# W_in converted by column groups with a scale each, block 0's gate projections moved into its attention, W_out converted in block 1

## The chip, the cores and the metric

The kernel runs on one core of one Trainium2 chip. The metric is the device time of one execution in microseconds, the median of several runs; lower is better. 3 runs of the kernel before stand at 1543.43 to 1545.45 us, with a median of 1544.86.

## The reference, cut to what matters

One layer of a decoder trunk over SEQ = 4096 tokens of width 1024: a norm, one input projection whose columns feed three mixers, gates, one output projection, a residual and a final norm.

```python
def rmsnorm(x, g):
    return x * rsqrt(mean(x * x, -1) + 1e-6) * g
...
h = rmsnorm(x, norm_g)                       # (4096, 1024)
proj = h @ w_in                              # 1024 x 2576
q_g, k_g, v_g, gk_lr, gate_g, u_p, gate_p, q_m, gate_m = split(proj)
gk = log_sigmoid(gk_lr @ w_gk_up + b_gk) / 16
o_gla = rmsnorm(gla_chunked(q_g, k_g, v_g, gk), gla_norm_g) * silu(gate_g)
o_pool = (multiscale_pool(u_p) @ pool_w per group) * pool_scale * silu(gate_p)
o_mem = memory_attention(q_m, rmsnorm(mem, mem_norm_g), w_mem_kv) * silu(gate_m)
x = x + concat(o_gla, o_pool, o_mem) @ w_out # 1024 x 1024
return rmsnorm(x, final_g)
```

gla_chunked is gated linear attention in chunks of 64 tokens, 4 heads; multiscale_pool is a trailing mean over 2, 4, 8 and 16 tokens; memory_attention attends to 256 memory tokens, 4 heads. All inputs and the output are float32.

## The kernel before, in words

**Numbers.** The large products run on float16 parts. A float32 matrix is scaled by a power of two, its float16 rounding is the high half, the rest is the low half, and three matmuls (high by high, high by low, low by high) replace one (`split`, L324 to L331). The scale comes from the largest entry: VectorE reduces along the columns, GpSimd's `partition_all_reduce` takes the largest over the partitions, and VectorE's `exponents` (L792) makes the scale and its inverse from the exponent bits.

**The head, L237 to L257, L293 to L322, L567 to L631, L807 to L853, L1115 to L1175.** SyncE issues all loads on one queue: the small vectors, the memory tokens and W_mem (1 and 2 MB), the transposed u columns of W_in, pool_w in four pieces, then W_in in eight slices of 128 rows. TensorE folds pool_w into the u columns. ScalarE squares the memory tokens, GpSimd adds the squares up, and VectorE scales the tokens. VectorE reduces each slice of W_in as it lands (L816) and, with the norm's weights `g_in` multiplied in (L828), one scale `s_w` for the whole of W_in comes out (L832). Only then ScalarE writes the high half of slice after slice (`hi_tile`, L593, 2560 columns each) and VectorE the low half (L852). The norm weights are part of the scaled W_in (`gs`, L837), so that x is only multiplied by its reciprocal root mean square. x of block 0 comes after the memory keys and values (L252 to L254), since `xb0` takes their buffer. W_out is loaded whole (4 MB, L257) when block 0's x has been split.

**The blocks.** 4096 tokens in 16 blocks of 256 (`TB`). `run_blocks` (L227) writes block 0 and block 15 out and runs blocks 1 to 14 in a loop, on each engine its own instruction stream; the order within an engine is the order of the code, and semaphores join the engines. TensorE's order in a block (L367): low-rank gate and q (L380, L384), decay logits (L388), k, v (L399), then `features` for the GLA gates, u, memory q, pool gate and memory gate (L403 to L411), 48 matmuls of 256 columns each; then the attention part: transposes and scores (L425, L435), memory scores (L452), states (L463), turns of the memory probabilities (L476), head outputs (L484, L490), memory values (L541), head norms (L498). Between the pieces of attention stand four quarters of the output projection of the block before (`quarter`, L501, `out_proj`, L345); block 0 has none. Within attention `rms_sum`, ScalarE's `rstd` and `x_parts`, VectorE's `normalise` (L799) and GpSimd's `x_lo_of` (L1137) make the next block's x.

**W_out in block 0.** VectorE reduces it (L940), GpSimd joins the partitions (L1171), and ScalarE (L679) and VectorE (L952) split it in eight slices, while TensorE runs block 0's projections. The raw copy `woraw` lies outside the buffers of the blocks.

**GpSimd's order** (L1114 on): constants, the memory tokens' sums (L1134), two all-reduces (L1149, L1151), the sums of x's squares, the low-rank weights (L1157 to L1161), x times its scale (L1164), the low half of x (L1143), memsets, the third all-reduce (L1171), memsets, then in each block the pooling sums (L1184 to L1191), the squares' sums and the low half of the next x.

```python
        def wait_split(eng, k):
            eng.wait_ge(hi_w, k + 1)
            eng.wait_ge(lo_w, k + 1)
```

Of the kernel before, what the change touches and what calls it, by code (L numbers as in the profile page):

```python
# [19 lines left out]
ALU = mybir.AluOpType  # L20
# [8 lines left out]
P = 128  # L29
D = 1024  # L30
# [40 lines left out]
O_TAIL = DIN * KT * 4  # L71


def hybrid_block(nc, xt, x, memt, w_in, w_ut, w_gk_up, vecs, pool_w, counts, w_mem, w_out, final_g, out):
    NB = xt.shape[0]
    ctx = ExitStack()
    with ctx:
# [21 lines left out]
        sca = sb("sca", [P, 34], F32)  # L99
# [5 lines left out]
        wmx = sb("wmx", [P, 2, KT], F32)  # L105
# [5 lines left out]
        g_in, g_mem, b_gk, g_out = vec[:, 0:8], vec[:, 8:16], vec[:, 16:18], vec[:, 18:26]  # L111
# [46 lines left out]
        wraw = view(0, [KT, DIN], F32)  # L158
        woraw = view(O_TAIL, [KT, D], F32)
        xb0 = view(O_TAIL, [KT, TB], F32)  # L160
        sq0 = view(O_TAIL + 8192, [KT, TB], F32)
        memb = view(O_TAIL, [KT, NMEM], F32)
        wmraw = view(O_TAIL + 8192, [KT, 512], F32)
        wflat = whl[:, :, :, :].rearrange("p a b c -> p (a b c)").bitcast(F32)
        wut = wflat[:, 0:2048].rearrange("p (a b) -> p a b", a=2)
        pwb = wflat[:, 2048:2304].rearrange("p (a b) -> p a b", a=2)
        msq = wflat[:, 2304:2304 + KT * NMEM].rearrange("p (a b) -> p a b", a=KT)
        rmem = wflat[:, 4608:4608 + NMEM]

        bank = [ctx.enter_context(nc.psum_tensor(f"bank{i}", [P, 512], F32)) for i in range(8)]  # L170
        kraw = bank[1][:, :].rearrange("p (a b) -> p a b", a=NPAIR)
        vraw = bank[2][:, :].rearrange("p (a b) -> p a b", a=MT)
# [3 lines left out]
        def col(n):  # L176
            return sca[:, n:n + 1]
        s_w, i_w, s_o, i_o, s_m, i_m, sc_in, sc_q, sc_out = (col(n) for n in range(9))
        s_vk, i_vk, e_vk, m_vk = (sca[:, n:n + 2] for n in (22, 24, 26, 28))
        s_v, s_k, i_v, i_k = (col(n) for n in (22, 23, 24, 25))  # L180
        sc_ms, sc_neg = col(30), col(31)
        gs = sca[:, 12:20]
        e_tmp = col(20)
        m_tmp = col(21)


        d_vec, d_mem, d_wut, d_wout, d_x, d_res, d_store = (
            sem(n) for n in ("d_vec", "d_mem", "d_wut", "d_wout", "d_x", "d_res", "d_store"))
        d_w = [sem(f"d_w{k}") for k in range(KT)]

        cleared, built, ident_ok, mem_sq, mem_sum, mem_ms, mem_ln, mem_r, mem_n = (
            sem(n) for n in ("cleared", "built", "ident_ok", "mem_sq", "mem_sum", "mem_ms", "mem_ln", "mem_r", "mem_n"))
        memk_done, memv_done, fold_done, fold_out = (
            sem(n) for n in ("memk_done", "memv_done", "fold_done", "fold_out"))
        max_in, max_all, hi_w, lo_w, hi_v, lo_v, hi_k, lo_k, hi_o, lo_o, scaled = (
            sem(n) for n in ("max_in", "max_all", "hi_w", "lo_w", "hi_v", "lo_v", "hi_k", "lo_k", "hi_o", "lo_o",
                             "scaled"))
        low_rank, qm_hi, qm_lo = (sem(n) for n in ("low_rank", "qm_hi", "qm_lo"))

        pe_lr, pe_q, pe_k, pe_logit, pe_v, pe_p2, pe_out, pe_ket, pe_sc, pe_ms, pe_st, pe_rb, pe_pt, pe_o, pe_msq, pe_pv = (  # L200
            sem(n) for n in ("pe_lr", "pe_q", "pe_k", "pe_logit", "pe_v", "pe_p2", "pe_out", "pe_ket", "pe_sc",
                             "pe_ms", "pe_st", "pe_rb", "pe_pt", "pe_o", "pe_msq", "pe_pv"))

        lr_out, abs_ok, expabs, softplus, eb_ok, enb_ok, ebl_ok, v_out, p2_out, y_sq, y_ln, y_r, x_sq = (
            sem(n) for n in ("lr_out", "abs_ok", "expabs", "softplus", "eb_ok", "enb_ok", "ebl_ok", "v_out",
                             "p2_out", "y_sq", "y_ln", "y_r", "x_sq"))
# [15 lines left out]
        def wait_split(eng, k):  # L222

            eng.wait_ge(hi_w, k + 1)
            eng.wait_ge(lo_w, k + 1)

        def run_blocks(eng, step, tail):  # L227

            step(0, True, False)
            with eng.Fori(1, NB - 1) as i:  # L230
                step(i, False, False)
            step(NB - 1, False, True)
            tail(NB)

        @block.sync
        def _(sp):
            sp.dma_start(vec[:, 0:26], vecs).then_inc(d_vec, 16)  # L237
            sp.dma_start(cnt[:, :, :], counts).then_inc(d_vec, 16)
            for g in range(P // RANK):
                sp.dma_start(up4[g * RANK:(g + 1) * RANK, :], w_gk_up).then_inc(d_vec, 16)  # L240
            sp.dma_start(fg[:, :], final_g.partition_broadcast(P)).then_inc(d_vec, 16)
            sp.dma_start(memb, memt).then_inc(d_mem, 16)
            sp.dma_start(wmraw, w_mem).then_inc(d_mem, 16)
            sp.dma_start(wut, w_ut).then_inc(d_wut, 16)
            sp.wait_ge(cleared, 1)
# [9 lines left out]
            sp.wait_ge(x_hi, 2)  # L255
# [996 lines left out]
```

## Time and profile before

| | |
|---|---|
| median of 3 runs | 1544.86 us (1543.43 to 1545.45) |
| the profiled execution, span | 1543.8 us |
| outside the span, median less span | 1.1 us |
| TensorE busy | 1443.0 us, 93% of the span |
| VectorE busy | 724.0 us, 47% |
| ScalarE busy | 608.1 us, 39% |
| GpSimd busy | 236.4 us, 15% |
| mean granted TensorE clock | 0.973 |
| read and written | 52.20 and 16.78 MB |

The span runs from the first to the last instruction of one profiled execution. PE is TensorE, PEld its weight loads, DVE VectorE, ACT ScalarE, POOL GpSimd, SP SyncE. A number in square brackets behind an instruction is the time its engine stood idle ahead of it, with what ended that; "issue" there is time in which the engine waited for nothing that the profile shows. A busy share is a mean over stages with different limits, so the stages are read one by one.

### The profile page before, as it was taken

What the parts mean: (1) busy time and instruction counts of PE and PEld (TensorE: products, weight loads), DVE (VectorE), ACT (ScalarE), POOL (GpSimd) and SP (SyncE); (2) the same over time, 40 slices, a digit from 0 to 9 for tenths busy, and PEclk for the clock granted to TensorE, in tenths of its full rate; (3) what the DMA queues carried; (4) which work ended last, traced back from release to release, by engine and by line L of the source; (5) the groups of instructions that cost most, each with busy time, mean ns of one, the idle gap of its engine ahead of it and who ended that gap; (6) DMA issues with size and microseconds to landing.
All of it is one profiled execution on the core that took longest, in us unless ns stands there. A gap on an engine that the chain in (4) does not pass through costs nothing.

```text
span 1543.8 us, 28261 instructions
## 1 busy us (share of the span) xinstructions
PE 1443.0 (93%) x11746; PEld 1046.2 (68%) x11746; DVE 724.0 (47%) x1221; ACT 608.1 (39%) x1101; POOL 236.4 (15%) x217
## 2 busy tenths in 40 slices
PE   3359699999999999999999999999999999999996
PEld 2238476776867677676867677686867767686762
DVE  2876625436172535527163544627163543616253
ACT  1344425344342534434252534434262534434241
POOL 1231201121110201121020202121020112112000
PEclk9669799999999999999999999999999999999998
DMA  8130100102010010102001010202001010201001
GB/s 337 65 136 1 42 2 28 54 0 82 0 69 12 27 54 10 71 0 82 0 36 46 27 54 0 82 0 82 0 27 54 21 61 0 82 0 46 10 28 68
DMA packets 15432, 69.32 MB, mean 45 GB/s; under 512 B 2352, under 2 KB 2480, under 8 KB 12848
## 3 DMA queue, kind: packets, MB, share of 16 engines
q1 hardware_dynamic: 15408, 68.98, 11.9%
q8 instruction: 18, 0.29, 0.1%
q14 instruction: 6, 0.05, 0.0%
HBM read 52.20 MB, written 16.78 MB: 45 GB/s over the span
## 4 chain that ended last, share of the span: by engine, by line
PE 90%; DVE 4%; ACT 2%; DMA 1%; issue 1%; POOL 1%; SPq 1%; DVEq 0%; ACTq 0%; POOLq 0%
PE bank L330 75%; PE bank L484 2%; PE bank L452 2%; PE bank L490 2%; PE bank L476 2%; PE bank L498 2%; DVE whl L852 1%; PE bank L541 1%; DVE wmx L816 1%; PE bank L463 1%; PE bank L388 1%; DMA whl<-in_pool_w 1%; PE bank L435 1%; PE bank L380 1%; POOL arena L1134 1%
## 5 line engine op out<-in xcount | busy, mean ns | idle before, releaser
L330 PE MATMUL bank<-arena,whl 128*128 128x256 f16 x6144 | 684.6, 274 | 2.6 <-DVE whl L852 2.6
L330 PEld LDWEIGHTS bank<-arena,whl 128*128 128x128 f16 x6144 | 602.3, 98 | 84.1 <-issue 6.5
L330 PE MATMUL bank<-arena 128*128 128x512 f16 x1536 | 344.1, 381 | 6.4 <-DVE arena L872 6.4
L330 PEld LDWEIGHTS bank<-arena 128*128 128x128 f16 x1536 | 147.8, 98 | 181.3 <-issue 15.4
L963 DVE SCALAR_TENSOR_TENSOR arena<-arena 64x256 f32<-64x256 f32 x60 | 25.2, 420 | 314.6 <-POOL arena L1191 313.2
L330 PE MATMUL bank<-whl,arena 128*128 128x512 f16 x768 | 168.3, 379 | 0.0
L686 ACT ACTIVATE arena<-bank,sca 128x512 f32<-128x512 f32 x64 | 43.9, 688 | 254.4 <-PE bank L330 253.3
L330 PEld LDWEIGHTS bank<-whl,arena 128*128 128x128 f16 x768 | 75.2, 99 | 86.9
L1143 POOL TENSOR_TENSOR arena<-arena 128x1024 f16<-128x1024 f32 x32 | 77.8, 2451 | 285.7 <-ACT arena L621 285.7
L1134 POOL TENSOR_TENSOR arena<-arena 128x1024 f32<-128x1024 f32 (+2 forms) x48 | 76.7, 1599 | 231.7 <-ACT arena L599 222.6
L1184 POOL TENSOR_TENSOR arena<-arena 128x542 f32<-128x542 f32 x16 | 17.4, 1090 | 606.1 <-ACT arena L693 598.3
L1001 DVE TENSOR_REDUCE mx<-bank 128x2 f32<-128x512 f32 x64 | 41.1, 683 | 138.4 <-PE bank L452 138.4
L1013 DVE SCALAR_TENSOR_TENSOR arena<-arena,rsum 128x256 f16<-128x256 f32 x128 | 62.3, 538 | 58.1 <-ACT arena L738 58.1
L883 DVE SCALAR_TENSOR_TENSOR arena<-bank,sca,arena 128x512 f32<-128x512 f32 x64 | 47.8, 749 | 79.8 <-DMA arena<-in_x 58.5
L728 ACT ACTIVATE arena<-bank,nm,sca 128x256 f32<-128x256 f32 x128 | 71.2, 560 | 4.0 <-ACT nm L718 2.4
L738 ACT ACTIVATE arena<-arena,rsum 128x256 f16<-128x256 f32 x128 | 56.1, 498 | 25.8 <-DVE rsum L1007 25.8
L671 ACT ACTIVATE arena<-bank,sca 128x512 f32<-128x512 f32 x32 | 22.0, 687 | 102.7 <-PE bank L330 102.7
L872 DVE SCALAR_TENSOR_TENSOR arena<-arena,sca 128x2048 f16<-128x2048 f32 x16 | 37.6, 2351 | 51.2 <-ACT arena L637 51.2
L643 ACT ACTIVATE arena<-arena 128x1024 bf16<-128x1024 f32 x32 | 33.6, 1050 | 55.5 <-DVE arena L883 55.5
L1038 DVE COPY arena<-bank 128x1024 f16<-128x1024 f16 x64 | 43.9, 687 | 16.3 <-PE bank L476 16.2
L700 ACT ACTIVATE arena<-bank 64x512 f16<-64x512 f32 x32 | 18.9, 592 | 73.3 <-PE bank L330 72.9
L763 ACT ACTIVATE arena<-bank,eps 128x512 f32<-128x512 f32 x32 | 21.7, 678 | 59.0 <-PE bank L498 59.0
(154 smaller groups left out, 1467.9 us busy)
## 6 DMA issues: line engine op xcount, KB each, us to landing
arena<-in_xt SPq DMA_DIRECT2D x16, 1024.0 KB, 5.2
arena<-in_x SPq DMA_DIRECT2D x32, 512.0 KB, 3.3
out<-arena SPq DMA_DIRECT2D x32, 512.0 KB, 2.6
arena<-in_w_in SPq DMA_DIRECT2D x8, 768.0 KB, 16.1
arena<-in_w_out SPq DMA_DIRECT2D x1, 4096.0 KB, 12.2
arena<-in_w_in SPq DMA_DIRECT2D x8, 392.0 KB, 16.2
arena<-in_w_mem SPq DMA_DIRECT2D x1, 2048.0 KB, 11.0
arena<-in_memt SPq DMA_DIRECT2D x1, 1024.0 KB, 6.6
```

Of the source, the lines that this page charges most:

```text
L330: mm = nc.tensor.matmul(ap, lhs, rhs, start=k == 0 and n == 0, stop=(k, n) == last)
L643: nc.scalar.activation(junk, yb, ACT.Square, accum_out=ysum[:, 0:1]).then_inc(y_sq, 1)
L686: nc.scalar.activation(gate[:, g:g + 2, :], bank[b][:, :].rearrange("p (a t) -> p a t", a=2), ACT.Silu, scale=sc_in).then_inc(p2_out, 1)
L728: a = nc.scalar.activation(pr[n % 2][:, h, :], bank[2 + n % 2][:, h * 256:(h + 1) * 256], ACT.Exp, bias=nm[:, 2 * n + h:2 * n + h + 1], sc ...
L738: a = nc.scalar.activation(phl[n % 2][:, 0, h, :], pr[n % 2][:, h, :], ACT.Copy, scale=rsum[:, 2 * n + h:2 * n + h + 1])
L872: nc.vector.scalar_tensor_tensor(mhl[:, 1, :, :], mixed, s_m, mhl[:, 0, :, :], ALU.mult, ALU.subtract).then_inc(m_lo, 1)
L883: nc.vector.scalar_tensor_tensor(yb[:, c], bank[h][:, :], sc_out, yb[:, c], ALU.mult, ALU.add).then_inc(y_add, 1)
L1001: nc.vector.tensor_reduce(mx[:, 2 * n:2 * n + 2], bank[2 + n % 2][:, :].rearrange("p (h m) -> p h m", h=2), AX.X, ALU.max).then_inc(max_ok, 1)
L1013: a = nc.vector.scalar_tensor_tensor(phl[n % 2][:, 1, h, :], pr[n % 2][:, h, :], rsum[:, 2 * n + h:2 * n + h + 1], phl[n % 2][:, 0, h, :], ...
L1038: nc.vector.tensor_copy(pt[:, p, :, t * P:(t + 1) * P], b16[b].rearrange("p (a b) -> p a b", b=P)).then_inc(pt_out, 1)
L1134: nc.gpsimd.tensor_tensor(buf[:, 0:half, :], buf[:, 0:half, :], buf[:, half:2 * half, :], ALU.add).then_inc(signal, 1)
L1143: nc.gpsimd.tensor_tensor(xn[:, 1, k, :], whole[:, k, :], xn[:, 0, k, :], ALU.subtract).then_inc(x_lo, 1)
```

## The change

Seven column groups of W_in (Q with the low-rank columns, K, V, memory Q, u, GLA gates, pool and memory gates) are seven inputs, loaded by one DMA each, reduced, scaled and split one by one. Each has its own scale, and each result is multiplied by its own inverse. The weights of the norm are no longer in W_in: `normalise` multiplies them into x, eight instructions on VectorE instead of one. The raw groups lie in buffers that the blocks use later, so that x of block 0 is loaded at once. The head's sums of squares move from GpSimd to VectorE. GpSimd takes the low halves of three groups, whose raw copy ScalarE scales in place first, and all-reduces each group's largest entry.

Block 0 no longer projects its four gates in the projection part: they stand at the places of the four quarters in its attention (`first_gate`), are copied out unscaled by silu (`raw_gate`), and one silu over all of them follows. W_out is loaded whole behind block 0's last weights for its largest entry alone, and in block 1, now written out as well (`second`), loaded again in eight tiles through two buffers that lie in `mixed`, and split there. The reserved size of a scratch area for DMAs, a build argument, is set to 2048.

```diff
-            for k in range(KT):
-                sp.dma_start(wraw[:, k, 0:CU], w_in[:, k, 0:CU]).then_inc(d_w[k], 16)
-                sp.dma_start(wraw[:, k, CGP:DIN], w_in[:, k, CU:DIN - 256]).then_inc(d_w[k], 16)
-            sp.wait_ge(memk_done, 1)
-            sp.wait_ge(memv_done, 1)
-            sp.dma_start(xb0, xt[0]).then_inc(d_x, 16)
...
+            sp.dma_start(memb, memt).then_inc(d_mem, 16)
+            sp.dma_start(wmraw, w_mem).then_inc(d_wmem, 16)
+            sp.dma_start(xb, xt[0]).then_inc(d_x, 16)
+            sp.dma_start(rq, w_q).then_inc(d_wq, 16)
+            sp.dma_start(rk, w_k).then_inc(d_wk, 16)
+            sp.dma_start(wut, w_ut).then_inc(d_wut, 16)
+            sp.dma_start(rv, w_v).then_inc(d_wv, 16)
+            sp.dma_start(rqm, w_qm).then_inc(d_wqm, 16)
+            sp.dma_start(rg, w_g).then_inc(d_wg, 16)
...
+            wait_weights(sp, GV)
+            sp.dma_start(rp, w_p).then_inc(d_wp, 16)
...
+                if first:
+                    wait_weights(sp, GG)
+                    wait_weights(sp, GP)
+                    sp.dma_start(woraw, w_out).then_inc(d_wout, 16)
+                if second:
+                    sp.wait_ge(m_lo, 1)
+                    for k in range(KT):
+                        if k >= 2:
+                            sp.wait_ge(hi_o, k - 1)
+                            sp.wait_ge(lo_o, k - 1)
+                        sp.dma_start(wotile[k % 2], w_out[:, k, :]).then_inc(d_tile[k % 2], 16)
```

On TensorE, in block 0, the fold of pool_w stands behind the logits, and the gates in attention:

```diff
+                if first:
+                    fold_pool()
+                    wait_weights(pe, GK)
...
+                def first_gate(n):
+                    if first:
+                        wait_weights(pe, GG if n < 2 else GP)
+                        if n >= 2:
+                            pe.wait_ge(gate_out, n - 1)
+                        features(n % 2, GATES[n]).then_inc(pe_g, 1)
 
                 mem_scores(0)
                 mem_scores(1)
...
                 quarter(0)
+                first_gate(0)
                 mem_scores(2)
                 mem_scores(3)
```

On ScalarE (in block 0's stream: Q, x, K, then V behind the low-rank copy, the fold's copies, U, the memory values, QM, GG, GP):

```diff
+            def weights_hi(g, c, raw, parts):
+                act.wait_ge(w_scaled, g + 1)
+                w, n = raw.shape[2], KT // parts
+                for h in range(parts):
+                    k = slice(n * h, n * (h + 1))
+                    a = nc.scalar.activation(whl[:, 0, k, c:c + w], raw[:, k, :], ACT.Copy, scale=sw[:, g:g + 1])
+                    if g in LO_POOL:
+                        a = nc.scalar.activation(raw[:, k, :], raw[:, k, :], ACT.Copy, scale=sw[:, g:g + 1])
+                    a.then_inc(hi_w, 1)
...
+                for k in range(3):
+                    out_hi(k)
+                if first:
+                    act.wait_ge(fold_done, 4)
+                    weights_hi(GG, CG, rg, 2)
+                else:
+                    silu(1, 2, 0)
+                    out_hi(3)
+                    out_hi(4)
+                    silu(2, 3, 2)
+                    out_hi(5)
+                    out_hi(6)
...
+                raw_gate(2)
+                raw_gate(3)
+                if first:
+                    act.wait_ge(gate_out, 4)
+                    nc.scalar.activation(gate, gate, ACT.Silu).then_inc(silu_ok, 1)
+                    nc.scalar.preload_act_table_set(EXP_LN)
```

On VectorE:

```diff
             def normalise(n):
                 dve.wait_ge(rb_ok, n + 1)
-                r = sq[:, 1:2, :].broadcast_to([P, KT, TB])
-                nc.vector.tensor_tensor(xb, xb, r, ALU.mult).then_inc(xn_ok, 1)
+                for k in range(KT):
+                    a = nc.vector.scalar_tensor_tensor(xb[:, k, :], xb[:, k, :], gx[:, k:k + 1], sq[:, 1, :],
+                                                       ALU.mult, ALU.mult)
+                    if k % (KT // 2) == KT // 2 - 1:
+                        a.then_inc(xn_ok, 1)
...
+                if first:
+                    dve.wait_ge(fold_out, 4)
+                    nc.vector.tensor_reduce(w_top[:, GU:GU + 1], ru, AX.XY, ALU.max,
+                                            apply_absolute_value=True).then_inc(w_max, 1)
+                    weights_scale(GQM, AR_QM)
...
+                    weights_scale(GU, AR_U)
+                    weights_max(GG, rg, d_wg)
+                    weights_lo(GU, CU, ru)
...
+                    weights_scale(GG, AR_GG)
+                    weights_max(GP, rp, d_wp)
+                    weights_scale(GP, AR_GP)
+                if second:
                     dve.wait_ge(d_wout, 16)
+                    after(nc.vector.tensor_reduce(wmx[:, :], woraw, AX.X, ALU.max, apply_absolute_value=True))
...
+                    dve.wait_ge(max_all, AR_WO)
                     exponents(mmax[:, 2:3], s_o, i_o)
+                    nc.vector.tensor_scalar(o_gain, o_gain, s_o, None, ALU.mult).then_inc(o_scaled, 1)
+                    dve.wait_ge(o_scaled, 1)
+                if not first:
+                    mixed_lo(i - 1)
+                if second:
                     for k in range(KT):
                         dve.wait_ge(hi_o, k + 1)
```

On GpSimd:

```diff
+            all_max(AR_G, sca[:, 87:88], g_top)
+            all_max(AR_Q, w_all[:, GQ:GQ + 1], w_top[:, GQ:GQ + 1])
             x_lo_of(0)
+            all_max(AR_K, w_all[:, GK:GK + 1], w_top[:, GK:GK + 1])
+            all_max(AR_V, w_all[:, GV:GV + 1], w_top[:, GV:GV + 1])
+            all_max(AR_KV, kvmax[:, 2:4], kvmax[:, 0:2])
...
+            all_max(AR_QM, w_all[:, GQM:GQM + 1], w_top[:, GQM:GQM + 1])
+            all_max(AR_U, w_all[:, GU:GU + 1], w_top[:, GU:GU + 1])
+            pool.wait_ge(fold_done, 4)
+            weights_lo(CQM, rqm, 0, KT, HI_DONE[GQM])
+            all_max(AR_GG, w_all[:, GG:GG + 1], w_top[:, GG:GG + 1])
+            weights_lo(CG, rg, 0, KT // 2, HI_DONE[GG] - 1)
+            weights_lo(CG, rg, KT // 2, KT, HI_DONE[GG])
+            all_max(AR_GP, w_all[:, GP:GP + 1], w_top[:, GP:GP + 1])
...
+                if second:
+                    all_max(AR_WO, mmax[:, 2:3], mmax[:, 0:1])
+                pool.wait_ge(u_out, i + 1)
...
+                if first:
+                    weights_lo(CGP, rp, 0, KT // 2, HI_DONE[GP] - 1)
+                    weights_lo(CGP, rp, KT // 2, KT, HI_DONE[GP])
```

## Rows read from the trace of the kernel before

**Rows 1.** The page: busy time of each engine, its share of the span, instructions

```profile
PE 1443.0 (93%) x11746; PEld 1046.2 (68%) x11746; DVE 724.0 (47%) x1221; ACT 608.1 (39%) x1101; POOL 236.4 (15%) x217
```

**Rows 2.** Busy time by stretch: PE, PEld, DVE, ACT, POOL, clock, DMA share, GB/s

```profile
0.00:92.00 92.00, 23.62 (x100) 20.12 (x100) 54.76 (x48) 32.67 (x26) 28.91 (x27) 0.75 0.43 169
92.00:185.50 93.50, 77.21 (x632) 59.31 (x633) 57.87 (x94) 38.63 (x66) 15.24 (x17) 0.88 0.14 57
273.00:361.00 88.00, 88.00 (x731) 63.92 (x730) 40.02 (x71) 35.74 (x67) 13.40 (x13) 1.00 0.10 36
```

**Rows 3.** Chain that ended last, 0 to 210 us: start, us, what

```profile
77.66 22.64 DVE whl L852 x6
```

**Rows 4.** Timeline of the head, 33 to 186 us: start, us, instructions, idle before

```profile
33.61 8.60 PE L307 MATMUL bank<-arena 128*128 128x256 f32 x32 [5.93 <-DVE arena L813]
...
154.36 1.03 PE L452 MATMUL bank<-kst,arena 128*128 128x256 f16 x8
...
185.49 0.62 PE L380 MATMUL bank<-arena,wlr 128*32 128x256 f16 x16 [3.77 <-POOL arena L1143]
```

**Rows 5.** Timeline around two turns of POOL's work

```profile
57.95 0.40 POOL L1151 PARTITION_ALL_REDUCE small<-small  x1 [6.22 <-DVE small L829]
58.23 1.91 ACT L599 ACTIVATE arena<-arena 128x2048 f32<-128x2048 f32 x1
65.01 7.97 POOL L1134 TENSOR_TENSOR arena<-arena 128x1024 f32<-128x1024 f32 x3 [6.66 <-issue]
...
125.08 0.41 POOL L1171 PARTITION_ALL_REDUCE small<-small  x1 [23.65 <-DVE small L943]
...
138.46 0.31 POOL L1175 MEMSET arena<- 128x256 f32 x1
138.64 0.69 ACT L693 ACTIVATE arena<-bank,sca 128x512 f32<-128x512 f32 x1
146.54 1.08 POOL L1184 TENSOR_TENSOR arena<-arena 128x542 f32<-128x542 f32 x1 [7.77 <-issue]
...
152.81 1.41 DVE L978 SCALAR_TENSOR_TENSOR arena<-bank,arena 64x512 f16<-64x512 f32 x2
```

**Rows 6.** Groups by line and form, DVE and POOL: busy us, mean ns, idle before

```profile
L872 DVE SCALAR_TENSOR_TENSOR arena<-arena,sca 128x2048 f16<-128x2048 f32 x16 | 37.6, 2351 | 51.2 <-ACT arena L637 51.2
L813 DVE SCALAR_TENSOR_TENSOR arena<-arena,vec,whl 128x256 f32<-128x256 f32 x8 | 3.3, 480 | 28.7 <-ACT whl L580 28.7
...
L1143 POOL TENSOR_TENSOR arena<-arena 128x1024 f16<-128x1024 f32 x32 | 77.8, 2451 | 285.7 <-ACT arena L621 285.7
L1164 POOL TENSOR_TENSOR arena<-arena 128x2048 f32<-128x2048 f32 x1 | 4.5, 4508 | 1.2 <-ACT arena L607 1.2
```

**Rows 7.** DMA issues: KB each, median us to landing

```profile
arena<-in_xt SPq DMA_DIRECT2D x16, 1024.0 KB, 5.2
arena<-in_x SPq DMA_DIRECT2D x32, 512.0 KB, 3.3
```

**Rows 8.** Timeline, block 0: the largest entry of W_out

```profile
115.45 9.10 DVE L940 TENSOR_REDUCE wmx<-arena 128x1 f32<-128x1024 f32 x8
```

**Rows 9.** Timeline: the end of block 14, and block 15 from its first matmul

```profile
1406.59 2.28 DVE L803 TENSOR_TENSOR arena<-arena 128x2048 f32<-128x2048 f32 x1
1409.76 2.00 ACT L621 ACTIVATE arena<-arena 128x1024 f16<-128x1024 f32 x2 [0.89 <-PE bank L541]
...
1416.59 0.62 PE L380 MATMUL bank<-arena,wlr 128*32 128x256 f16 x16
1434.61 1.99 ACT L637 ACTIVATE arena<-arena,sca 128x2048 f16<-128x2048 f32 x1
1439.00 31.60 PE L330 MATMUL bank<-arena,whl 128*128 128x256 f16 x288
1461.32 1.41 DVE L978 SCALAR_TENSOR_TENSOR arena<-bank,arena 64x512 f16<-64x512 f32 x2
1471.60 1.05 PE L452 MATMUL bank<-kst,arena 128*128 128x256 f16 x8
```

More of the change, by code:

```diff
@@ L269, in outputs, with step @@
                 sp.dma_start(out[rows, :], yb).then_inc(d_store, 16)
-            def step(i, first, last):
+            def step(i, first, second, last):
                 if not last:
@@ L291, in _ @@
         def _(pe):
-            pe.wait_ge(d_wut, 16 * 5)
-            for k in range(KT):
-                for g in range(2):
-                    mm = nc.tensor.matmul(bank[4 + k // 2][:, (k % 2) * 256 + g * P:(k % 2) * 256 + g * P + P],
-                                          wut[:, g, k * P:(k + 1) * P], pwb[:, g, :], start=True, stop=True)
-            mm.then_inc(fold_done, 1)
             pe.wait_ge(built, 3)
@@ L580, in _ @@
             nc.scalar.activation(rmem, rmem, ACT.Exp, scale=-0.5).then_inc(mem_r, 1)
-            act.wait_ge(memk_done, 1)
-            act.wait_ge(memv_done, 1)
-            act.wait_ge(scaled, 1)
-            nc.scalar.activation(vm[:, 0, :, :], vraw, ACT.Copy, scale=s_v).then_inc(hi_v, 1)
-            for h in range(2):
-                r = slice(64 * h, 64 * h + 64)
-                for half in range(2):
-                    nc.scalar.activation(kst[64 * half:64 * half + 64, :, h, 0, :], kraw[r, :, :], ACT.Copy,
-                                         scale=s_k[r, :]).then_inc(hi_k, 1)
@@ L648, in norm_y, with step @@
                 nc.scalar.activation(yr[:, 0:1], yr[:, 1:2], ACT.Exp, scale=-0.5).then_inc(y_r, 1)
-            def step(i, first, last):
-                if first:
-                    wait_split(act, KT - 1)
+            def step(i, first, second, last):
                 act.wait_ge(pe_lr, i + 1)
@@ new lines, in _ @@
+            fold_rows(0, mem_sum)
+            dve.wait_ge(mem_r, 1)
+            for m in range(KT):
+                nc.vector.scalar_tensor_tensor(memb[:, m, :], memb[:, m, :], g_mem[:, m:m + 1], rmem,
+                                               ALU.mult, ALU.mult).then_inc(mem_n, 1)
+            dve.wait_ge(x_sq, 1)
+            fold_rows(0, sq_add)
+            weights_max(GQ, rq, d_wq)
+            weights_scale(GQ, AR_Q)
+            normalise(0)
+            dve.wait_ge(hi_w, HI_DONE[GQ])
@@ L893, in _, with step @@
                 nc.vector.memset(nm[:, n:n + 1], 0.0).then_inc(y_add, 1)
-            def step(i, first, last):
+            def step(i, first, second, last):
                 dve.wait_ge(pe_logit, i + 1)
@@ L1224 @@
     q, k, v, lr, gg, u, gp, qm, gm = np.split(w, np.cumsum(sizes)[:-1], axis=1)
+    blocks = np.zeros((P, 2, P), np.float32)
+    for g in range(4):
+        h = 64 * (g % 2)
+        blocks[h:h + 64, g // 2, h:h + 64] = a["pool_w"][g]
     counts = np.zeros((P, 2, HALO), np.float32)
```

604 lines of the change are left out of this document (344 added, 260 removed).

## The prediction, made before the changed kernel ran

> **What bounds the kernel now.** I read the page's busy shares first. TensorE is busy for 93% of the span, no other engine for half [rows 1]. The stretches show where the missing part lies: in a middle block TensorE works 88.0 of 88.0 us at full clock, while it works 23.6 us in the first 92 and 77.2 in the 93.5 after those [rows 2]. So the loop has nothing to give, and the head has about 85 us of idle TensorE. The chain of waits says whose they are: its longest piece there is VectorE's, six slices of the low half of W_in's split, each over all 2560 columns [rows 3]. One scale for the whole of W_in means that block 0 waits for every byte of it. Block 0's first matmuls stand at 92 us, its attention begins at 154.36, block 1 at 185.49 [rows 4].
>
> The third view is GpSimd's timeline, and it speaks against the change. After the all-reduce that ends at 58.35 the next elementwise instruction has its input at 60.14 (squares), yet starts at 65.01, with an idle of 6.66 us put down to "issue". After the third all-reduce (only memsets lie between) the same: input at 139.33, start at 146.54, idle 7.77 [rows 5]. So this GpSimd pays 6.7 to 7.8 us of its own idle time in turning from an all-reduce to elementwise work. The Trainium skill (GPSIMD Engine Reference, section 2.1, Instruction dispatch) gives a reason: a freshly loaded kernel costs about 6 us of code load, with no visible instruction. The trace agrees, at 6.7 and 7.8 us.
>
> **What the change does to that.** Before there are three all-reduces, and two turns back whose cost shows. After there are ten. In GpSimd's new program order the kinds alternate: memsets, all-reduces G and Q, x_lo of block 0, all-reduces K, V, KV, QM, U, low half of QM, GG, low half of GG, GP, the pooling sums, WO, the sums of block 1. That is five turns to elementwise work and five to all-reduces. The turn to an all-reduce has no price: the last one before lay behind 23.65 us of idle time [rows 5]. Its bounds are 0 and 7.8 us; the nearest row is the other turn, so I take 6.7 for both.
>
> **Head and block 0, in milestones** (us from the start). Durations by 2048 elements per partition: ScalarE 1.9 to 2.0 [rows 5, 9], VectorE 2.35 with two inputs [rows 6] and 2.3 for a largest entry (9.10 for 8192, [rows 8]), GpSimd 4.2 to 4.5 [rows 6]; a scale (four tiny operations and one more) 0.8, an estimate.
> 1. Memory tokens land near 6, x near 14, the weights by 34: 12 MB at the rate of x's landings, 1 MB in 5.2 with the start-up and 2.5 more each after that, an estimate [rows 7]. Transfers no longer set anything.
> 2. All-reduce G comes with its turn at 10.7, and VectorE waits for it ahead of everything. Memory squares folded on VectorE 14.7, norm 16.4, memory scaled (8 times 0.41, [rows 6]) 19.7, memory keys on TensorE (8.6, [rows 4]) 28.4, x's norm 30.5, x normalised in two halves 33.9.
> 3. x_lo on GpSimd, 2.45 each [rows 6] from 34 on, and slower beside VectorE's split of Q (estimate), ends at 41. Block 0 starts at 41 instead of 92.
> 4. Turn to K's all-reduce: 48.1. Then K and V scales 51, the low-rank copy, logits 52.5, the split of K and V 61 (V's two halves on VectorE 4.7), TensorE's W_u fold in four steps between ScalarE's copies 61, K's features to 68, the decays and keys 70, U's largest entry 72.4, its scale 74.4.
> 5. ScalarE: high halves of U, memory values, v, QM in two passes: 84.5. GpSimd's low half of QM 88.9. Here GpSimd becomes the path: turn 95.6, all-reduce GG and scale 96.8, turn, two low halves of 4.25 from 102.7 to 111.2, turn, all-reduce GP 118.3, turn 125.0, pooling sums, pooled and query low half 7.7 (146.54 to 154.22, [rows 5]): block 0's attention starts at 132.7 instead of 154.36. VectorE stands behind the wait for GP's all-reduce in its queue, so nothing of attention can pass it. TensorE is idle from about 97.
> 6. Attention before took 31.1 us from there to block 1 [rows 4]. Now the four gate projections stand in it: 192 of the 288 matmuls in 31.60 us [rows 9], 21.1, and 3 for a cold clock after the idle stretch (estimate). Waits of the old attention hide some 16 of these; the silu over all of gate, with two table loads between the last gate and x's split, puts 4.5 back. My sum by steps is 43: block 1 starts at 175.7. **Gain 9.8 us.**
>
> **Block 1.** W_out (4 MB) is read whole once in block 0's attention and again in eight tiles of 512 KB; 4 MB more on a queue that is idle. Its largest entry, 9.1 us [rows 8], with all-reduce and scales 11.8, now stands ahead of the mixed scale, so ScalarE's mixed high half moves from 18.0 us after the block's start (1434.61 less 1416.59, [rows 9]) to 27.5, and the buffer that the tiles need is free at 32. The turn to the all-reduce is covered, as GpSimd waits 25 us there. Two buffers for eight tiles: a round is landing 3.3 [rows 7], ScalarE 1.05, VectorE 1.25 (half of 2.35), waits 0.2: 5.8. Four rounds end at 58.4; ScalarE's copy of u stands behind the seventh tile, at 55. Pooling and query low half follow at 62.1; as before they end at 46.1 (1461.32 and 1.41 less 1416.59), and TensorE asks for them at 55.0 (1471.60 less 1416.59, [rows 9]). **Loss 7.1 us**, since a middle block has no idle TensorE time to win it back.
>
> **Every block.** Normalising x is 8 instructions of 0.41 instead of one of 2.28: 1 us more of VectorE. At the end of block 14 it runs from 1406.59 and ScalarE takes x at 1409.76 behind TensorE [rows 9]; the first half would be there at 1408.3, the second at 1409.9, needed at 1410.8. Cost nothing; without that cover 1 us in 15 blocks. The gain vector and group scales change operands only. One block more is written out, one pass of the loop less: nothing, within 0.5 us.
>
> **Sum.** 9.8 less 7.1 is 2.7 off the profiled 1543.8, 1541.1. The median, 1544.86, is 1.1 above that execution, so 1542.2, and I forecast **1542**. A measurement of this kernel can tell about 0.2%, 3.1 us, from no change, so this is just inside it. By the Trainium skill's 6 us a turn (GPSIMD Engine Reference, section 2.1), six turns on the path would cost 4 us less, an estimate.
>
> **Rivals.**
> - Turns to an all-reduce are cheap (bound 0). G then saves 4.1 (memory squares are there at 8), K 2.6 (VectorE is busy to 45.5), GG and GP 6.7 each: 20.1 less, 1522. If turns hid wholly, 8.5 more: 1513.6. For it: no all-reduce before shows the cost. Against: two of two turns back do. Chance 0.30.
> - Block 1's tile ring sets the end, slower than before. If tiles land as x's megabytes do, 5.2 instead of 3.3 [rows 7], four rounds give 7.6 more: 1549.8. It decides from a round of 7.3 us on. For it: each load waits for two engines' marks; against: W_out's tiles are alone on the queue. Chance 0.25.
> - The change does not do what it says in block 1: the conversion hides, with the round under 4 us. 1535. Chance 0.05.
> - The forecast, 0.40, range by itself 1535 to 1548 (turns of 6.0 to 7.8, attention 40 to 46).
>
> **Numbers.** Range 1512 to 1553: it takes in the cheap turns and the slow ring with 3 us of steps mis-sized. Faster by over 0.2%: the cheap turns, the hidden conversion and 0.15 of the forecast, 0.50. Within: 0.20. Slower: the ring and 0.05, 0.30.
>
> **What would show it.** In the timeline of the changed kernel: block 0's first matmul near 41, GpSimd idle of 6 to 8 us with "issue" at each of the alternations, about 35 us of idle TensorE ahead of the first memory scores at 133, block 1 at 176, and in block 1 its memory scores at 62 us after the block's start instead of 55. All-reduces that start at once behind elementwise work make the first rival right; attention that begins before 115 or block 1 before 160 makes the forecast wrong, as does a middle block over 88 us.

## The result and the profile after

The changed kernel takes 1556.37 us, the median of 4 runs (1552.85 to 1556.92), against 1544.8 for the kernel before beside it: 1.0071 of it, with a 95% interval of 1.0059 to 1.0083. The forecast was 1542, with a range of 1512 to 1553: the sign was wrong and the range missed. The page of the profile after, its span, its busy shares and the landing times of W_out (whole, then in eight tiles: KB each, median us):

```profile
span 1554.5 us, 28138 instructions
...
PE 1440.8 (93%) x11746; PEld 1043.6 (67%) x11746; DVE 743.7 (48%) x1362; ACT 618.8 (40%) x1110; POOL 239.0 (15%) x219
...
arena<-in_w_out SPq DMA_DIRECT2D x1, 4096.0 KB, 12.2
arena<-in_w_out SPq DMA_DIRECT2D x8, 512.0 KB, 3.8
```

The shares hardly differ from [rows 1]. A share over 1554 us can't show 10 us, so the next view is that of the stretches (PE, PEld, DVE, ACT, POOL, clock, DMA share, GB/s), as in [rows 2]:

```profile
0.00:50.00 50.00, 24.35 (x129) 19.68 (x130) 25.34 (x47) 10.99 (x12) 9.12 (x21) 0.97 0.69 270
50.00:92.00 42.00, 31.51 (x208) 22.30 (x206) 32.81 (x52) 21.96 (x24) 6.40 (x6) 0.92 0.20 76
92.00:146.00 54.00, 6.78 (x78) 5.44 (x76) 22.26 (x28) 20.17 (x16) 25.23 (x14) 0.58 0.17 68
146.00:190.00 44.00, 39.32 (x364) 32.32 (x363) 23.25 (x48) 22.25 (x45) 5.15 (x4) 0.89 0.11 37
190.00:280.00 90.00, 80.83 (x668) 59.25 (x666) 51.35 (x84) 39.19 (x66) 9.92 (x10) 0.96 0.20 63
280.00:368.00 88.00, 88.00 (x730) 63.83 (x729) 40.95 (x78) 35.72 (x68) 13.24 (x13) 1.00 0.10 37
```

TensorE now works 55.9 of the first 92 us where it worked 23.6, so the early start is real. Then comes a hole from 92 to 146 us with 6.8 us of work, and block 1 (most of it in the row from 190 to 280 us, 80.8 of 90.0) is no longer full. A middle block still works 88.0 of 88.0 (last row). Where the stages begin, on TensorE's timeline (L406 is the first matmul of a block, L495 the first memory scores; start, duration, idle before and its releaser):

```profile
43.00 0.98 PE L406 MATMUL bank<-arena,wlr 128*32 128x256 f16 x16 [4.19 <-POOL arena L1311]
...
143.39 1.89 PE L495 MATMUL bank<-kst,arena 128*128 128x256 f16 x8 [47.22 <-DVE arena L1141]
...
152.20 1.04 PE L495 MATMUL bank<-kst,arena 128*128 128x256 f16 x8
...
183.98 1.05 PE L406 MATMUL bank<-arena,wlr 128*32 128x256 f16 x16 [3.77 <-issue]
...
251.21 1.89 PE L495 MATMUL bank<-kst,arena 128*128 128x256 f16 x8 [8.08 <-DVE arena L1141]
...
285.74 0.62 PE L406 MATMUL bank<-arena,wlr 128*32 128x256 f16 x16
...
1427.35 0.62 PE L406 MATMUL bank<-arena,wlr 128*32 128x256 f16 x16
```

Block 0's projections start 49 us earlier than before, and block 1 only 1.5 us earlier (183.98 for 185.49 of [rows 4]). Block 2 starts at 285.74 where it started at 274.98, and block 15 at 1427.35 for 1416.59 [rows 9]: 10.76 us both times. So blocks 2 to 15 cost what they did, and the span's 10.7 us are 1.5 won in the head and block 0 against 12.3 lost in block 1, which is 101.76 us long instead of 89.49. Normalising x in each block is hidden, as foretold.

Eight matmuls of the memory scores take 1.89 us right behind a hole and 1.04 nine microseconds later. In the hole's stretch the granted clock is 0.58, near the lower of its two levels (1.2 of 2.4 GHz).

**The head's hole.** A turn is GpSimd's change from an all-reduce to elementwise work or back. Its timeline shows both:

```profile
13.11 0.41 POOL L1317 PARTITION_ALL_REDUCE sca<-sca  x1 [9.33 <-issue]
...
48.65 0.76 POOL L1317 PARTITION_ALL_REDUCE sca<-sca  x2 [5.91 <-issue]
...
94.81 0.41 POOL L1317 PARTITION_ALL_REDUCE sca<-sca  x1 [5.87 <-issue]
102.64 8.07 POOL L1323 TENSOR_TENSOR whl<-arena,whl 128x2048 f16<-128x2048 f32 x2 [7.42 <-issue]
116.75 0.41 POOL L1317 PARTITION_ALL_REDUCE sca<-sca  x1 [6.05 <-issue]
124.27 1.08 POOL L1355 TENSOR_TENSOR arena<-arena 128x542 f32<-128x542 f32 x1 [7.11 <-issue]
...
128.02 8.32 POOL L1323 TENSOR_TENSOR whl<-arena,whl 128x2048 f16<-128x2048 f32 x2
136.30 4.63 POOL L1303 TENSOR_TENSOR arena<-arena 128x1024 f32<-128x1024 f32 x3
```

The alternation costs about what was put down: 5.9 to 6.05 us of idle time before an all-reduce (9.33 before the very first), 7.1 to 7.4 before elementwise work. Up to the pooling sums at 124.27 (forecast: 125.0) the head is on time. The miss comes in the next 19 us, on VectorE:

```profile
128.09 4.01 DVE L1130 TENSOR_TENSOR arena<-arena,cnt 64x16 f32<-64x16 f32 x1 [10.06 <-POOL arena L1362]
132.03 0.39 DVE L1132 SCALAR_TENSOR_TENSOR arena<-arena 64x240 f32<-64x240 f32 x1
132.34 4.02 DVE L1135 TENSOR_TENSOR arena<-arena 64x16 f32<-64x16 f32 x1
136.39 2.27 DVE L1130 TENSOR_TENSOR arena<-arena,cnt 64x16 f32<-64x16 f32 x1
...
141.92 1.41 DVE L1141 SCALAR_TENSOR_TENSOR arena<-bank,arena 64x512 f16<-64x512 f32 x2
```

L1130 and L1135 make the first columns of the means, 64 partitions by 16 elements. Such an instruction takes 0.17 us when alone (experiments below), and here 4.01, 4.02 and 2.27. Two kinds of GpSimd work run beside them. Beside the first two it is the low half of group GP, two instructions in 8.32 us, 4.16 each. Beside the third it is the sums of squares of block 1's x (L1303), three instructions in 4.63 us, the first of 2.33. Two more of VectorE's instructions meet the rest of these sums: 1.24 us for 0.17, and 0.93 for 0.40. Together that is 7.7 us beside the low half and 3.7 beside the sums. The query's low half, and with it TensorE, comes 10.7 us later than forecast.

**Block 1.** One timeline, VectorE, GpSimd, SyncE's queue and ScalarE:

```profile
202.43 8.67 DVE L1103 TENSOR_REDUCE wmx<-arena 128x8 f32<-128x8192 f32 x1
...
213.60 2.00 ACT L703 ACTIVATE arena<-arena,sca 128x2048 f16<-128x2048 f32 x1 [8.69 <-DVE sca L990]
...
228.21 1.15 ACT L755 ACTIVATE arena<-arena,vec 128x1024 f16<-128x1024 f32 x1 [4.08 <-DMA arena<-in_w_out]
...
234.63 1.15 ACT L755 ACTIVATE arena<-arena,vec 128x1024 f16<-128x1024 f32 x1 [2.23 <-DMA arena<-in_w_out]
...
242.60 1.60 POOL L1355 TENSOR_TENSOR arena<-arena 128x542 f32<-128x542 f32 x1 [30.55 <-ACT arena L787]
...
245.12 1.33 DVE L1116 SCALAR_TENSOR_TENSOR arena<-arena,vec 128x1024 f16<-128x1024 f32 x1 [1.86 <-ACT arena L755]
```

From the block's start: the mixed high half at 29.6 us (18.0 in [rows 9]), because 8.67 us of W_out's largest entry stand ahead of its scale; the first tile's load at 34.0; the tiles of one buffer 6.4 apart (228.21 to 234.63); the last low half ends at 62.5; and the memory scores stand at 67.2, with 8.08 us of idle TensorE. In block 15 of the kernel before they stood at 55.0, in its block 1 at 56.7 (242.17). So 10.5 us of the 12.3 are lost up to the scores, and 1.8 behind them: after the idle stretch the scores take 1.89 us for 1.04 and the next 24 matmuls 6.26 for 5.35.

### The profile page after: what moved, and what is told of

Its sections match the earlier page's. It is cut to its first block, busy times and chain, and to the rows that moved or that the text cites. A ratio compares the mean times of both kernels' runs of the same rounds, so it can differ in the third digit from the quotient of the medians.

```text
span 1554.5 us, 28138 instructions
## 1 busy us (share of the span) xinstructions
PE 1440.8 (93%) x11746; PEld 1043.6 (67%) x11746; DVE 743.7 (48%) x1362; ACT 618.8 (40%) x1110; POOL 239.0 (15%) x219
## 4 chain that ended last, share of the span: by engine, by line
PE 84%; issue 5%; DVE 4%; ACT 2%; POOL 2%; DMA 2%; DVEq 0%; POOLq 0%; ACTq 0%; SPq 0%
PE bank L358 70%; PE bank L495 2%; PE bank L519 2%; PE bank L527 2%; PE bank L533 2%; PE bank L541 2%; PE bank L600 1%; PE bank L506 1%; DMA arena<-in_w_out 1%; PE bank L416 1%; POOL whl L1323 1%; PE bank L329 1%; PE bank L478 1%; PE bank L406 1%; POOL arena L1311 1%
## 5 line engine op out<-in xcount | busy, mean ns | idle before, releaser
L1311 POOL TENSOR_TENSOR arena<-arena 128x1024 f16<-128x1024 f32 x32 | 73.8, 2327 | 318.1 <-ACT arena L659 318.1
L1303 POOL TENSOR_TENSOR arena<-arena 128x1024 f32<-128x1024 f32 (+2 forms) x45 | 68.8, 1529 | 207.9 <-ACT arena L642 205.6
L1176 DVE SCALAR_TENSOR_TENSOR arena<-arena,rsum 128x256 f16<-128x256 f32 x128 | 61.2, 530 | 56.3 <-ACT arena L842 56.3
L495 PE MATMUL bank<-kst,arena 128*128 128x256 f16 x256 | 35.0, 282 | 55.3 <-DVE arena L1141 55.3
L495 PEld LDWEIGHTS bank<-kst,arena 128*128 128x128 f16 x256 | 23.6, 100 | 63.7 <-DVE arena L1141 55.6
```

The lines of the kernel that those rows point to most:

```text
L495: mm = nc.tensor.matmul(bank[b][:, h * NMEM:(h + 1) * NMEM], qst[:, p, h, t * P:(t + 1) * P], kst[:, p, h, r, :], start=r == 0, stop=r == 1)
L1176: a = nc.vector.scalar_tensor_tensor(phl[n % 2][:, 1, h, :], pr[n % 2][:, h, :], rsum[:, 2 * n + h:2 * n + h + 1], phl[n % 2][:, 0, h, :], ...
L1303: nc.gpsimd.tensor_tensor(sq[:, 0:half, :], sq[:, 0:half, :], sq[:, half:2 * half, :], ALU.add).then_inc(sq_add, 1)
L1311: nc.gpsimd.tensor_tensor(xn[:, 1, k, :], xb[:, k, :], xn[:, 0, k, :], ALU.subtract).then_inc(x_lo, 1)
```

## The experiments

Each is an edit of the changed kernel. Ratios are to the kernel before, timed beside them on the same chip (1544.2 to 1545.3 us), with 95% intervals; "less" or "more" without a word is against the 1556.37 of the change. Milestones of one and the same head move by about 1 us from execution to execution (block 0 starts at 42.5 to 44.4 where the head is unchanged).

**GpSimd's low half of GP kept away from VectorE's small instructions.**

```diff
                 if first:
+                    pool.wait_ge(pooled, 4)
+                    pool.wait_ge(qm_lo, 2)
                     weights_lo(CGP, rp, 0, KT // 2, HI_DONE[GP] - 1)
```

> GpSimd starts the low half of the gate weights GP only when VectorE's pooled and query low half of block 0 are done. Theory (VectorE's tiny two-input instructions stand behind GpSimd's long ones, 4.0 us each): the stretch from the end of the pooling sums to the first memory scores falls from 15.3 us to about 4, attention of block 0 starts near 132.5 instead of 143.4, and as GP's low halves then end near 141, before the third gate asks, the whole is 10 to 11 us faster than the changed kernel, about 1545.5. Rival (those instructions are slow for another reason, as code fetch or a first use): the stretch stays at 15 us, and GP's low halves come later: 1556 or more.

1544.01 us, 0.9993 [0.9984, 1.0003]: 12.4 less, where 10 to 11 were expected. The timeline of this run:

```profile
129.12 0.17 DVE L1130 TENSOR_TENSOR arena<-arena,cnt 64x16 f32<-64x16 f32 x1 [9.98 <-POOL arena L1362]
...
133.02 1.89 PE L495 MATMUL bank<-kst,arena 128*128 128x256 f16 x8 [36.80 <-DVE arena L1141]
133.09 8.10 POOL L1323 TENSOR_TENSOR whl<-arena,whl 128x2048 f16<-128x2048 f32 x2 [4.00 <-issue]
...
138.78 5.19 DVE L1176 SCALAR_TENSOR_TENSOR arena<-arena,rsum 128x256 f16<-128x256 f32 x2 [0.97 <-ACT arena L842]
```

The same instruction takes 0.17 us for 4.01, the scores stand at 133.02 (the forecast said 132.7), and block 1 starts at 172.73. No arithmetic was taken out: two waits on GpSimd brought back all that the change lost. They stand ahead of the low half of GP, and so hold back the sums of squares behind it too; the last version below holds back the sums alone. The stall moved on in part: a pair of two-input instructions of attention (L1176), 0.88 us in the changed kernel, now takes 5.19. The first of the pair, 2.70, ends with the low half, the second with the first of the sums.

**W_out's largest entry reduced in block 0**, behind the normalising of block 1's x, where VectorE has time.

```diff
                 if second:
-                    dve.wait_ge(d_wout, 16)
-                    after(nc.vector.tensor_reduce(wmx[:, :], woraw, AX.X, ALU.max, ...))
...
+                if first:
+                    dve.wait_ge(d_wout, 16)
+                    after(nc.vector.tensor_reduce(wmx[:, :], woraw, AX.X, ALU.max, ...))
                 rows(2)
```

> The largest entry of W_out is reduced on VectorE in block 0, behind the normalising of block 1's x, where VectorE waits for the silu, and no longer ahead of the mixed scale in block 1. Theory (the 8.7 us reduction and its all-reduce push the tile ring of block 1 back by 11 us): the mixed high half moves from 29.6 to 18 us after block 1's start, the memory scores of block 1 from 67.2 to 55 to 57, and 10 to 12 us go: about 1545. Rival (the ring's own length sets it): a ring that starts 11 us earlier and still ends late, under 5 us gained.

1544.45 us, 0.9996 [0.9986, 1.0005]: 11.9 less. The 10 to 12 us that were expected came. Block 1 starts at 184.25, near the 183.98 without the edit, takes 91.7 us for 101.8, and its scores wait 1.11 us instead of 8.08:

```profile
205.00 1.99 ACT L703 ACTIVATE arena<-arena,sca 128x2048 f16<-128x2048 f32 x1
...
243.16 1.05 PE L495 MATMUL bank<-kst,arena 128*128 128x256 f16 x8 [1.11 <-DVE arena L1136]
```

**A third buffer for W_out's tiles** (`yb`, free at that point), the ring otherwise the same; behind the last tile the load queue waits until the sixth is split.

```diff
-        wotile = [view(O_MIX + 4096 * b, [D], F32) for b in range(2)]
+        wotile = [view(O_MIX + 4096 * b, [D], F32) for b in range(2)] + [yb]
...
-                        if k >= 2:
-                            sp.wait_ge(hi_o, k - 1)
-                            sp.wait_ge(lo_o, k - 1)
+                        if k >= 3:
+                            sp.wait_ge(hi_o, k - 2)
+                            sp.wait_ge(lo_o, k - 2)
```

> W_out's tiles go through three buffers instead of two; the largest entry stays where it is. Theory (a round of landing 3.8, ScalarE 1.16, VectorE 1.29 and waits for two tiles sets the ring, 26 us): the ring ends about 7 us earlier, memory scores of block 1 at 60 to 62 us after its start instead of 67.2, 5 to 7 us gained: about 1550. Rival (ScalarE's queue, with two silus and a table load among the tiles, or the DMA queue sets the ring): under 2 us.

1549.01 us, 1.0025 [1.0014, 1.0036]: 7.4 less, slightly over the 5 to 7 expected. Block 1 takes 95.3 us, its scores wait 3.25. Both the late start of the ring and its round are on the path, then: either one mended takes most of the wait away, and together (below) they take all of it.

**An extra pair of turns**, and **the same two instructions without a turn**. Both stand behind GP's all-reduce:

```diff
             all_max(AR_GP, w_all[:, GP:GP + 1], w_top[:, GP:GP + 1])
+            nc.gpsimd.tensor_tensor(idle[:, 2:3], eps[:, 0:1], eps[:, 1:2], ALU.add)
+            nc.gpsimd.partition_all_reduce(small[:, 15:16], g_top, P, RMAX)
```

> Adds to GpSimd's order, between the all-reduce of GP and the pooling sums of block 0, one one-element addition and one all-reduce whose results nobody reads: one turn to elementwise work and one back more. Theory (each turn costs 5.9 to 7.4 us on the path): the pooling sums start 12 to 14 us later, and so does everything: about 1569. Rival (the idle time ahead of these instructions is a wait for something else, or turns close together cost once): under 3 us more, 1557 to 1559.

1569.33 us, 1.0157 [1.0140, 1.0174]: 13.0 more, for 0.6 us of work. The GpSimd timeline:

```profile
117.61 0.41 POOL L1317 PARTITION_ALL_REDUCE sca<-sca  x1 [5.97 <-issue]
124.75 0.18 POOL L1346 TENSOR_TENSOR small<-eps 128x1 f32<-128x1 f32 x1 [6.73 <-issue]
130.74 0.41 POOL L1347 PARTITION_ALL_REDUCE small<-sca  x1 [5.80 <-issue]
138.11 1.08 POOL L1357 TENSOR_TENSOR arena<-arena 128x542 f32<-128x542 f32 x1 [6.96 <-issue]
```

The control has the two lines in the other order (the all-reduce first), so that all-reduce follows all-reduce and elementwise follows elementwise:

> The control to the run with two extra turns: the changed kernel with the same two instructions more, the all-reduce directly behind GP's all-reduce and the one-element addition directly ahead of the pooling sums, so that the number of turns stays. Theory (the turn costs, not the instructions): 0 to 1 us more than the changed kernel, 1556 to 1558. Rival (the instructions themselves cost): 1562 or more.

1556.11 us, 1.0071 [1.0056, 1.0087]: the change's own time. So the price hangs on the alternation, not on the two instructions, and even one element per partition brings it.

**All-reduces GG and GP moved ahead of QM's low half**, three elementwise halves behind them: two turns fewer each way.

```diff
-            pool.wait_ge(fold_done, 4)
-            weights_lo(CQM, rqm, 0, KT, HI_DONE[GQM])
             all_max(AR_GG, w_all[:, GG:GG + 1], w_top[:, GG:GG + 1])
+            all_max(AR_GP, w_all[:, GP:GP + 1], w_top[:, GP:GP + 1])
+            pool.wait_ge(fold_done, 4)
+            weights_lo(CQM, rqm, 0, KT, HI_DONE[GQM])
             weights_lo(CG, rg, 0, KT // 2, HI_DONE[GG] - 1)
             weights_lo(CG, rg, KT // 2, KT, HI_DONE[GG])
-            all_max(AR_GP, w_all[:, GP:GP + 1], w_top[:, GP:GP + 1])
```

> GpSimd's order alone is changed: the all-reduces of GG and GP stand directly behind those of QM and U, ahead of its low halves, so that one turn to elementwise work is left where there were two, and one turn back less by two. Theory (the turns are the path of block 0 from 89 to 124 us): the all-reduce of GP near 91 instead of 117, pooling sums end near 114 instead of 128, first memory scores 15 to 24 us earlier (GpSimd's low half of GP then falls beside VectorE's small instructions), 1532 to 1541. Rival (the path there is ScalarE's two passes or VectorE's queue): under 5 us, 1551 or more.

1540.31 us (1535.33 to 1544.22), 0.9968 [0.9954, 0.9982]: 16 less, and 0.3% less than before, within the 1532 to 1541 expected.

```profile
91.67 0.36 POOL L1317 PARTITION_ALL_REDUCE sca<-sca  x1 [8.74 <-DVE sca L913]
98.94 12.10 POOL L1323 TENSOR_TENSOR whl<-arena,whl 128x2048 f16<-128x2048 f32 x3 [6.90 <-issue]
...
115.61 8.27 POOL L1323 TENSOR_TENSOR whl<-arena,whl 128x2048 f16<-128x2048 f32 x2 [0.81 <-ACT arena L669]
115.85 4.04 DVE L1135 TENSOR_TENSOR arena<-arena 64x16 f32<-64x16 f32 x1
119.92 3.99 DVE L1130 TENSOR_TENSOR arena<-arena,cnt 64x16 f32<-64x16 f32 x1
```

The pooling sums end at 114.8 instead of 128: half of what four turns cost, about 26 us, is gained. GP's all-reduce now waits for VectorE's largest entry until 91.67, and only behind it and a turn comes the low half of QM, at 98.94 instead of 84.87. The scores stand at 130.16, 13.2 us earlier for the 15 to 24 expected: the collision with the low half of GP came along, in the same sizes.

**All low halves on VectorE.** ScalarE's second, scaling pass over QM, GG and GP goes with it, and GpSimd does all-reduces alone until the pooling sums.

```diff
-LO_DVE = {GQ: 1, GK: 2, GV: 4, GU: 5}
-LO_POOL = {GQM: 1, GG: 3, GP: 5}
+LO_DVE = {GQ: 1, GK: 2, GV: 4, GU: 5, GQM: 6, GG: 8, GP: 10}
+LO_POOL = {}
```

with GpSimd's `weights_lo` calls moved to VectorE's stream.

> All low halves are VectorE's, none GpSimd's; ScalarE's second pass over QM, GG and GP falls away, and GpSimd's all-reduces follow each other without a turn. Theory (turns, plus GpSimd's 4 us for what VectorE does in 2.35, plus the two engines in each other's way): first memory scores near 109 instead of 143, block 1 near 150 instead of 184, 1518 to 1526. Rival (VectorE, now with six more of 2.35 us in its queue, becomes the path): scores at 120 or later, 1533 or more.

1527.26 us, 0.9882 [0.9865, 0.9898]: 29 less, just short of the 1518 to 1526 expected. The scores stand at 115.43 for the 109 expected, block 1 starts at 155.95 for 150. The collision shows in both directions, here at GpSimd's pooling sums beside VectorE's low halves, then at VectorE's first small instruction beside GpSimd's sums of squares:

```profile
101.29 1.85 POOL L1356 TENSOR_TENSOR arena<-arena 128x542 f32<-128x542 f32 x1 [6.90 <-issue]
103.21 3.01 POOL L1358 TENSOR_TENSOR arena<-arena 128x538 f32<-128x538 f32 x1
...
107.80 2.29 DVE L1135 TENSOR_TENSOR arena<-arena,cnt 64x16 f32<-64x16 f32 x1 [2.52 <-POOL arena L1363]
```

The first two are 1.08 us each in the changed kernel's head, and one of VectorE's low halves beside them takes 3.18 us where alone it takes 2.35.

**Versions put together.** First this edit with the early largest entry and the third tile:

> The low halves on VectorE, the largest entry of W_out in block 0, and three tile buffers in block 1. Theory (the losses of block 0 and block 1 are separate and add up, the early entry alone takes nearly all that three buffers would): the low-on-vector time less 10 to 12 us, 1508 to 1514. Rival (the earlier W_out load or reduction now delays block 0's end, where VectorE has less room): a sum that falls short by 5 us or more, 1518.

1515.81 us, 0.9814 [0.9797, 0.9830]: 11.5 less than the version before it, as expected from the difference, though outside the 1508 to 1514 that were named. Block 1 now takes 87.8 us (156.03 to 243.84), less than the 89.49 of before, and its scores don't wait. Then the first gate projection ahead of the memory scores, where TensorE is idle, and the small scale of the norm weights behind the memory tokens instead of ahead of them:

```diff
+                if first:
+                    pe.wait_ge(u_out, 1)
+                first_gate(0)
                 mem_scores(0)
                 mem_scores(1)
```

> As the one before, and two orders more: block 0's first gate projection stands ahead of the memory scores, where TensorE is idle, and the other three move up one place; VectorE takes the norm weights' scale behind the memory tokens instead of ahead of them, where it waits for the first all-reduce until 13.1 us. Theory (both places are on the path): the first TensorE work at 14 instead of 17 us, block 0 starts 4 to 5 us earlier, attention of block 0 takes 4 to 5 us less; 1500 to 1506. Rival (block 0's head is set by other waits, and the gates filled idle time in attention anyway): no more than 2 us under the one before.

1508.07 us, 0.9759 [0.9743, 0.9775]: 7.7 less than the version before it, where 1500 to 1506 was expected. Block 0 starts at 38.60, its scores stand at 111.31. Last, GpSimd's sums of squares for block 1's x wait in block 0 for the pooled query, as in the first experiment:

```diff
+                if first:
+                    pool.wait_ge(pooled, 4)
+                    pool.wait_ge(qm_lo, 2)
                 if not last:
                     pool.wait_ge(x_sq, i + 2)
```

> As b8, and in block 0 GpSimd adds up the squares of block 1's x only when VectorE's pooled and query low half are done. Theory (the two engines hold each other up, here 4.63 us of GpSimd beside VectorE's small instructions): pooled and query low half together fall from about 7.7 to 4 us, first memory scores 3 to 4 us earlier, 1503 to 1506. Rival (the sums then fall beside VectorE's work of the first memory probabilities, and give it back): 1507 to 1509.

1506.14 us (5 runs, 1505.10 to 1506.55), 0.9745 [0.9731, 0.9758]: 2.5% faster than before and 3.2% than the change, at the upper edge of the 1503 to 1506 expected. Its scores, and its second stretch:

```profile
96.27 2.07 POOL L1361 TENSOR_TENSOR arena<-arena 128x542 f32<-128x542 f32 x1 [6.91 <-issue]
...
106.90 1.89 PE L497 MATMUL bank<-kst,arena 128*128 128x256 f16 x8 [4.94 <-DVE arena L1145]
```

```profile
50.00:110.00 60.00, 43.93 (x316) 32.00 (x315) 53.03 (x72) 27.99 (x33) 14.17 (x13) 0.87 0.29 114
```

From the end of the pooling sums (102.97) to the scores it is now 3.9 us for 7.7 in the version before, so the sums of squares alone were worth 3.7 there. The scores come 4.4 us earlier, but the kernel gains only 1.9: from the scores to block 1 it takes 40.4 us for 37.9, so that part of the rival came too. TensorE waits 4.00 us ahead of the first gate and 4.94 ahead of the scores, where it waited 47.22. VectorE is busy for 53 of these 60 us, but the path to the scores still runs through GpSimd: a turn of 6.91 us, then the pooling sums, the first two of them lengthened to 2.07 and 3.01 beside VectorE's low halves.

## Why the prediction was wrong

The forecast's sum ended at a span of 1541.1; it is 1554.5, and the 13.4 us between are two terms.

**The gain, 9.8 forecast, 1.5 measured.** Milestones 1 to 4 and the first part of 5 held: block 0 at 43.0 (41), all-reduce K at 48.65 (48.1), GP at 116.75 (118.3), pooling sums at 124.27 (125.0). Block 0's start was in part luck: the low half of x began 3.8 us late, behind a first all-reduce at 13.11 for 10.7, and took 5.0 us for 7. The step that failed is in milestone 5, "pooling sums, pooled and query low half 7.7". It measured 19.1 (124.27 to 143.39). The 7.7 was read off [rows 5], where nothing else ran on GpSimd behind the sums. In the new program order the low half of GP stands there, and behind it the sums of squares of block 1's x. The prediction lists GpSimd's order to count its turns; both make no turn, both are left out there, and it never asked what runs on VectorE beside them. With both held back the scores stand at 133.02. Attention then took 40.6 us for the 43 forecast, which gave 2.4 back, and the sums had started 0.7 early: 9.8 less 11.4, plus 3.1, is 1.5. In attention the 3 us for a cold clock, an estimate, were about right: the scores take 1.89 us for 1.04 and the first gate 7.30 for 5.40, 2.8 together.

**The loss, 7.1 forecast, 12.3 measured.** The mechanism was right and three sizes were small: the ring starts at 34.0 us into the block for 32; landings take 3.8 us for 3.3 and a round 6.4 for 5.8, so that the ring takes 28.4 us for 26.4; pooling and the query's low half take 4.8 for 3.7, since GpSimd's sums (1.60 for 1.08) run beside VectorE's last tiles. Together that is 5.1 us. (Four rounds of 5.8 are 23.2; where the other 3.2 of the forecast's 26.4 come from, it doesn't say.) That these close the gap is in part luck: the forecast measured from block 15's scores at 55.0, where block 1 of the kernel before had them at 56.7, and it had no term for the 1.8 us that TensorE loses behind the wait.

**The rivals.** Cheap turns to an all-reduce fell: three of them show 5.87 to 6.05 us in the changed kernel, and the extra pair cost 13.0. The Trainium skill (GPSIMD Engine Reference, section 2.1, Instruction dispatch) gives about 6 us for loading the code of a fresh kernel, and the size fits these turns; the turn back is 0.7 to 1.4 us above it. The page doesn't say that a turn is such a load: that is the prediction's reading, and no run here tests it. The tile ring as the end, slower than before, had the right sign and place, but its mechanism (landings of 5.2 us, a round over 7.3) didn't come: the round is 6.4. By itself the loss of block 1 would have been balanced by the gain, as the first experiment shows, which ends at the time of before with block 1's loss still in it. So neither case named the cause. For the stretch that failed the range, 1553, took in no collision between the engines; milestone 3 had allowed for one, at the low half of x.

The collision could be seen in the trace of the kernel before. At the end of its block 0 an instruction of VectorE that has a median of 0.68 us (L1044) runs beside a GpSimd instruction of 2.12 us:

```profile
183.18 2.62 DVE L1044 TENSOR_TENSOR arena<-arena 128x512 f32<-128x512 f32 x1 [2.58 <-ACT arena L766]
```

A rule that bears on this was not weighed. The Trainium skill (SBUF — State Buffer, section SBUF: two separate sides) says that VectorE and GpSimd share one pair of ports, which one instruction holds for all of its duration while the other engine's is fully blocked, and that VectorE's instructions with two SBUF inputs are among those that need it. The runs agree in size: 4.01 us beside instructions of 4.16. That the ports are the reason is the skill's statement; the runs show only that removing the neighbours removes the wait.

## What to carry to other kernels

- Write down GpSimd's whole new program order and count how often it goes from an all-reduce to elementwise work and back: about 13 us a pair here, wherever no longer wait hides it. Put the all-reduces next to each other.
- For each short VectorE instruction on the path, ask what GpSimd does at that moment. Here a stage's duration read from the old trace didn't hold with new neighbours; two waits that keep them apart were worth 12 us.
- Work moved into a block whose TensorE is full must end before its consumer asks. Place the part that others wait for (here a reduction) in a block with idle time, even if the bulk stays where it is.

## What the runs showed of the hardware

- A VectorE instruction of 64x16 elements with two inputs took 0.17 us alone, 4.0 us beside a GpSimd elementwise instruction of 4.1 to 4.3 us, and 2.27 beside one of 2.33. A pair of 128x256 took 0.88 us alone and 5.19 where it met two GpSimd instructions. GpSimd's 1.08 us instruction took 3.01 beside VectorE's low halves. In none of these cases did the short instruction end before the long one beside it, so the loss went by the neighbour's length, not by its own.
- GpSimd's turn cost 5.7 to 6.5 us to an all-reduce in the head and 6.7 to 7.8 back (8.7 once) wherever its input was ready, and nothing between instructions of one kind. Ahead of W_out's all-reduce in block 1 it was 7.4 to 8.0, in the four runs where the early largest entry leaves it bare. Behind a longer wait it didn't show: the low half of QM starts at 84.87, 0.15 us after its input. The first all-reduce of the kernel showed 8.8 to 10.9 us of idle time over the runs; in that stretch of the changed kernel the DMA share is 0.69. Whether the loads slow it was not tried.
